# Seven more blocks and one recurrence result of a two-layer fp32 kernel turned by VectorE and ScalarE instead of TensorE

## The chip, the cores and the metric

The kernel runs on one core of a Trainium2 chip. The metric is the device time of one execution in microseconds (us). Before the change it is 2432.59 us, the median of three runs (2432.58 to 2432.67).

## What is computed

A sequence of 256 tokens with 2048 features passes through two layers, all in fp32. The first layer is a gated recurrence beside a short convolution, an output projection, and a feed-forward part. The second is conditioned by a vector (`ada`) and has two attentions, an output projection and a feed-forward part. Cut to what matters here:

```
# first layer
proj = rms(x) @ w_in                    # q, f forward, f backward, i, gate, b, c, h: 1024 columns each
y_rec  = rms(recurrence(silu(q), gates(f forward), gates(f backward), i)) * hgrn_norm_w * silu(gate)
y_conv = b * conv3(c * h)
x = x + concat(y_rec, y_conv) @ w_out ;  x = x + ffn(x) ;  x = rms(x)
# second layer
proj = h @ w_in_2                       # c_q (512), c_kv (512), k_pe (64), q_sb, k_sb, v_sb, two gates
q  = (rms(c_q) * g_q_latent) @ w_uq     # 8 heads of 128 "nope" and 64 "rope" columns
kv = (rms(c_kv) * g_kv_latent) @ w_ukv  # 8 heads of 128 k_nope and 128 v
y_a = attention(rms(q) * g_q_head, rms(k) * g_k_head, v)     # with rope on the 64 columns
y_b = stick_breaking(q_sb, k_sb, v_sb)
x = x + gt1 * ((sigmoid(gl_a) * (y_a @ w_mla) + sigmoid(gl_b) * (y_b @ w_sb)) @ w_out_2) ;  x = x + gt2 * ffn(x)
```

## The kernel before

**The stream of weights.** Every large product is cut into blocks of 512 output columns, each block into chunks of 256 rows of its weight (a chunk is 128 partitions x 1024 numbers, two rows of tiles). A chunk comes by DMA into one of four `raw` buffers. ScalarE (ACT) rounds it to fp32r in `cast` (L994, tile `whi`), VectorE (DVE) computes what the rounding left in `low` (L1418, `wlo`), and TensorE (PE) multiplies in `products` (L957 to L959): for each of two row tiles and two token halves `hi*whi + hi*wlo + lo*whi`, 12 matmuls of 512 columns. One such chunk on PE is a **visit**; there are 913, numbered from 0. Each engine runs one instruction stream written out by hand. Slot s of a stream belongs to visit s: PE does `side_work(s)` and then the products of visit s, ACT does its `side_work(s)` and then the cast of chunk s+3, DVE the low part of that chunk at the start of its slot s+1, before its own `side_work(s+1)`. So between the slot in which a chunk is cast and the visit that needs it lie three visits. Nothing is reordered at run time; a late instruction delays all behind it on its engine.

**Turning.** A finished block lies with tokens on partitions; for the next product or attention it must have features there. Two ways are in use. On PE: `turn` (L664), a transposition of 128 x 128, 8 for a block, into PSUM, from where ACT and DVE read it. Without PE, for blocks that `is_far` names: `turned` on DVE (L1759), two STREAM_TRANSPOSE of 128 x 512, which turn each square of 32 x 32 in itself, into the rows of `between(b)`; then 16 copies of 32 partitions x 256 (`piece`, L1035 on ACT, L1506 on DVE), which put the squares in their places in `features_at(b)`. `pace(b)` says how many pieces a slot has on ACT and on DVE, (3, 0) as a rule. `live(s)` gives the blocks whose side work is due: `t` counts slots from the end of the block, up to `LIFE`.

**The places of this change.** Visits 16 to 23 are the block `fb` (the backward gate's input) of group 0 of the recurrence; its half steps follow in `hgrn(g, u)`, where u counts slots from `H0[g]` (slot 30 for group 0, 94 for group 1), with seven levels three slots apart; its result is normed, gated and turned at u = 33 to 37 and used by block `out` from visit 128 on. Visits 428 to 447 are the two latent blocks of the second layer; 457 to 462 the blocks `uqr` and `nope` q0, q1; 471 to 474 `nope` k0, k1; 475 to 478 the values `uv`; from 479 on the four blocks `heads` of the second attention. A `nope` block is evacuated at t = 0 (L1150), squared at t = 1 (L1156), summed at t = 2 (L1690 and after), scaled by its norm at t = 4 (L1712), turned at t = 6 and scaled by its gain as ACT takes it out of PSUM (L1163). The first attention's head h has its scores at slot `MLA0 + 3h`, that is from slot 485 on.

```
def cast(c):                      # ACT
    if pl.after[c] is not None:
        e.wait_ge(*visit(pl.after[c]))       # the visit that frees the buffer
    ...
    e.copy(whi[i][:, :, :], raw[u % RAW][:, 2 * hf:2 * hf + 2, :])
for s in range(SLOTS):            # ACT
    side_work(s)
    for c in pl.visits[s][2]:
        cast(c)
```

Of the kernel before, what the change touches and what calls it, by code (L numbers as in the profile page):

```python
# [29 lines left out]
LIFE = 14  # L30
# [262 lines left out]
def two_block_kernel(nc, a, out):  # L293
    ctx = ExitStack()
    with ctx:
# [221 lines left out]

        def as_features(t):

            return flat(t).rearrange("p (k s) -> p k s", k=4)  # L520
# [24 lines left out]
        H0 = [pl.end("fb", g) + 6 for g in range(2)]  # L545
# [3 lines left out]
        MLA0 = pl.begin("heads", "qs", 0) + 6  # L549
# [18 lines left out]
        FAR = (("fup", None), ("sb", 3), ("out", 3), ("heads", None), ("q", None), ("ff", None), ("h", 1), ("b", 1))  # L568
# [25 lines left out]
        def between(b):  # L594

            if b.kind in ("fup", "sb", "out"):
                return FT[:, :, :]
            if b.kind == "heads":
                return gl[0][:, :, :] if b.arg == ("ks", 1) else T2[1 - b.index % 2][:, :, :]
            k0 = 8 if (b.kind, b.arg[0]) == ("ff", 0) else 12  # L600
            return way[k0][:, :, :]

        def features_at(b):

            n = b.arg[-1]
            if b.kind in ("fup", "sb", "out"):
                return as_features(T2[n % 2][:, :, :])
            if b.kind == "heads":
                return (qs if b.arg[0] == "qs" else ks)[:, 4 * n:4 * n + 4, :]
            if b.kind == "q":  # L610
                return qT[:, :].rearrange("p (k s) -> p k s", k=4)
            if b.kind == "ff":
                return Kx[:, 0, :].rearrange("p (k s) -> p k s", k=4)
            if b.kind == "h":
                return U[:, :, 1:S + 1]
            return bT[:, :, :]
# [6 lines left out]

        def piece(b, q, i):

            d = features_at(b)[32 * q:32 * q + 32, :, :].rearrange("p k (m i c) -> p m i k c", m=2, i=4)
            r = between(b)[32 * i:32 * i + 32, :, :].rearrange("p m (k q c) -> p m q k c", k=4, q=4)
            return d[:, :, i, :, :], r[:, :, q, :, :]
# [33 lines left out]
        def tensor_program(e):  # L662
# [18 lines left out]
            def block_side(b, t):  # L681
# [20 lines left out]
                elif kind == "kpe" and t == 1:  # L702
                    e.wait_ge(*acc_read(b, 0))
                    o = next_bank(e, b.index)
                    for m in range(2):
                        ins = turn(o[:, P * m:P * m + P], ev_tmp(b, 0)[:, P * m:P * m + P])
                    ins.then_inc(*ev("pe_turn", b.index))
                elif kind == "nope" and t == 6:
                    for m in range(2):
                        e.wait_ge(*on("dve_nope", b.index, "scaled", m))  # L710
                        turn_tokens(b, m, (b.index, m))
                elif kind == "heads" and t == 2:
                    for m in range(2):
                        e.wait_ge(*acc_read(b, m))
                        turn_tokens(b, m, (b.index, m))
                elif kind == "sb" and t in (2, 3):
                    m, j = t - 2, b.arg[0]
                    e.wait_ge(*on("dve_merge", j, m))
                    o = next_bank(e, b.index, m)
                    for k in range(4):  # L720
                        ins = turn(o[:, P * k:P * k + P], ffn_tmp(j, m)[:, P * k:P * k + P])
                    ins.then_inc(*ev("pe_turn", b.index, m))

            def hgrn(g, u):
# [34 lines left out]
                elif u in (35, 36):  # L759
# [49 lines left out]
            def side_work(s):  # L809
# [10 lines left out]
                for g in range(2):  # L820
                    if 0 <= s - H0[g] < 40:
                        hgrn(g, s - H0[g])
# [61 lines left out]
            def left_here(b, i, ci, m):  # L884
# [5 lines left out]
                elif b.kind == "out" and b.arg == (0,) and i == 0 and m == 0:  # L890
                    if kt < 8:
# [18 lines left out]
                elif (b.kind == "uqr" or b.kind == "nope" and b.arg == ("k", 0)) and i == 0 and m == 0:  # L910
                    e.wait_ge(*side_read(pl.at["latent", 0 if b.kind == "uqr" else 1].index, ci))
# [60 lines left out]
        def scalar_program(e):  # L972
# [38 lines left out]
            def block_side(b, t):  # L1011
# [18 lines left out]
                elif is_far(b) and 2 <= t < settled(b):  # L1030
                    if t == 2:
                        for m in range(2):
                            e.wait_ge(*on("dve_turned", b.index, m))
                    for q, i in pieces(b, t, "act"):
                        ins = e.copy(*piece(b, q, i))  # L1035
                    if last_piece(b, t, "act"):
                        ins.then_inc(*ev("act_moved", b.index))
                elif is_far(b) and kind == "ff" and t == settled(b):
                    e.wait_ge(*on("act_moved", b.index))
                    e.activation(TA[:, 1024:2048], Kx[:, 0, :], ACT.Sigmoid, bias=0.0, scale=1.0).then_inc(  # L1040
                        *ev("act_gate", b.index, "f"))
                    e.activation(Kx[:, 0, :], Kx[:, 0, :], ACT.Sigmoid, bias=0.0, scale=-1.0).then_inc(
# [6 lines left out]
                elif is_far(b) and kind == "out" and t in (8, 9):  # L1049
                    half, k0 = t - 8, 4 * b.arg[0]  # L1050
                    if half == 0:
                        await_moves(e, b)
                    for k in (2 * half, 2 * half + 1):
                        ins = e.activation(hH[:, k0 + k, :], features_at(b)[:, k, :], ACT.Copy, bias=0.0,
                                           scale=vc("ffn_norm_w", k0 + k))
# [4 lines left out]
                elif is_far(b) and t >= 2 and kind != "out":  # L1060
# [97 lines left out]
                elif kind == "nope" and t == 6:  # L1158
# [19 lines left out]
                elif kind == "gl" and t == (3 if b.arg[0] == 3 else 0):  # L1178
                    i = b.arg[0]
                    e.wait_ge(*visit(end))  # L1180
                    if i == 0 and is_far(pl.at["heads", "ks", 1]):
                        await_moves(e, pl.at["heads", "ks", 1])
# [19 lines left out]
            def hgrn(g, u):  # L1202
# [21 lines left out]
                elif u in (35, 36):  # L1224
# [27 lines left out]
            def side_work(s):  # L1252
                for b, t in live(s):
                    block_side(b, t)
                for g in range(2):
                    if 0 <= s - H0[g] < 40:
# [141 lines left out]
        def vector_program(e):  # L1398
# [97 lines left out]
            def block_side(b, t):  # L1496
                kind, end = b.kind, pl.last[b.index, 1]
                t -= late0(b)
                if is_far(b) and t == 1:
                    turned(b)  # L1500
                elif is_far(b) and 2 <= t < settled(b) and pace(b)[1]:
                    if t == 2:
                        for m in range(2):
                            e.wait_ge(*on("dve_turned", b.index, m))
                    for q, i in pieces(b, t, "dve"):
                        ins = e.tensor_copy(*piece(b, q, i))  # L1506
                    if last_piece(b, t, "dve"):
                        ins.then_inc(*ev("dve_moved", b.index))
                elif is_far(b) and kind in ("fup", "sb") and t == settled(b) + 1:
# [3 lines left out]
                elif is_far(b) and kind == "out" and t in (9, 10):  # L1513
                    half, k0 = t - 9, 4 * b.arg[0]
                    e.wait_ge(*on("act_half", b.index, half))
                    for k in (2 * half, 2 * half + 1):
                        ins = e.scalar_tensor_tensor(hL[:, k0 + k, :], features_at(b)[:, k, :], vc("ffn_norm_w", k0 + k),
                                                     f(hH[:, k0 + k, :]), ALU.mult, ALU.subtract)
# [131 lines left out]
                elif kind == "latent" and t == 5:  # L1650
# [94 lines left out]
            def turned(b):  # L1745

                for m in range(2):
                    if b.kind == "sb":
                        e.wait_ge(*on("dve_merge", b.arg[0], m))
                    elif b.kind == "out":  # L1750
                        e.wait_ge(*on("dve_x1", b.index, m))
                    else:
                        e.wait_ge(*acc_read(b, m))
                if (b.kind, b.arg) == ("heads", ("ks", 1)):
                    e.wait_ge(*on("pe_head", "mla", 7, "y"))
                elif b in users:
# [79 lines left out]
            def hgrn(g, u):  # L1836
# [52 lines left out]
                elif u in (36, 37):  # L1889
# [204 lines left out]
            def side_work(s):  # L2094
# [4 lines left out]
                for g in range(2):  # L2099
                    if 0 <= s - H0[g] < 40:  # L2100
# [280 lines left out]
```

## Time and profile before

| | |
|---|---|
| median of three runs | 2432.59 us |
| the profiled execution | 2432.96 us |
| its span, first to last instruction | 2431.1 us |
| PE busy | 2424.0 us, 11540 matmuls |
| DVE busy | 1794.2 us |
| ACT busy | 1411.8 us |
| granted clock of PE | 1.00 |
| PE in the chain that ended last | 99% |

The profiled execution takes 1.9 us more than its span: what lies before the first and after the last instruction. Matmuls overlap in the pipeline, so that one of 512 columns is shown as 379 ns long while the next starts 216 ns after it; PE's speed is read from starts. The engines' busy shares are averages over the whole program.

### The profile page before, as it was taken

The page shows a single profiled execution, that of the slowest core. Times are in us where ns is not written, and L with a number is a line of the kernel's source. Part 1 is how long each engine was busy: PE and PEld are TensorE (multiplying, and loading weights), DVE is VectorE, ACT ScalarE, POOL GpSimd, SP SyncE. Part 2 cuts the span into 40 slices and gives each one's busy share as a digit, 9 for nine tenths or more (in the row PEclk, how much of TensorE's full clock was granted, in tenths as well). Part 3 has the DMA queues.
Part 4 walks back from the last instruction along what each step waited for, and adds up shares of the span by engine and source line. Part 5 has one row for each costly group of instructions (what it writes and reads, how often), then busy time and mean ns, then how long its engine had stood idle before and what let it go on. Part 6 is the DMA issues. An engine that isn't in the chain of part 4 may idle for free.

```text
span 2431.1 us, 29441 instructions
## 1 busy us (share of the span) xinstructions
PE 2424.0 (100%) x11540; PEld 2125.4 (87%) x11540; DVE 1794.2 (74%) x2231; ACT 1411.8 (58%) x1980; POOL 26.0 (1%) x27
## 2 busy tenths in 40 slices
PE   9999999999999999999999999999999999999999
PEld 8898888888888888888888888888888888888888
DVE  7888798777778778786666666789778775555555
ACT  7647645756654455655766664465656564455643
POOL 0000000000000000000010000000000000000000
PEclk9999999999999999999999999999999999999999
DMA  8656667787778877786455456878577776556564
GB/s 306 242 193 233 234 213 254 247 292 274 271 267 311 308 263 276 271 291 218 168 190 173 163 173 241 291 254 298 190 277 278 278 275 208 202 199 205 203 205 146
DMA packets 83321, 582.38 MB, mean 240 GB/s; under 512 B 9712, under 2 KB 10096, under 8 KB 13552
## 3 DMA queue, kind: packets, MB, share of 16 engines
q1 hardware_dynamic: 83040, 580.39, 67.2%
q8 instruction: 91, 1.49, 0.2%
q14 instruction: 46, 0.38, 0.0%
q10 hardware_dynamic: 144, 0.12, 0.0%
HBM read 578.36 MB, written 2.11 MB: 239 GB/s over the span
## 4 chain that ended last, share of the span: by engine, by line
PE 99%; DMA 0%; DVE 0%; ACT 0%; SPq 0%; issue 0%; POOL 0%; ACTq 0%
PE bank L957 32%; PE bank L958 32%; PE bank L959 32%; PE bank L738 1%; PE bank L664 1%; DMA raw<-in_w_in_dram 0%; PE bank L776 0%; PE bank L787 0%; PE bank L788 0%; PE bank L757 0%; PE bank L746 0%; PE bank L756 0%; PE bank L777 0%; PE bank L804 0%; PE bank L940 0%; PE bank L941 0%
## 5 line engine op out<-in xcount | busy, mean ns | idle before, releaser
L1418 DVE TENSOR_TENSOR wlo<-raw,whi 128x1024 fp32r<-128x1024 f32 x885 | 1077.5, 1221 | 554.2 <-ACT whi L994 550.0
L994 ACT CAST whi<-raw 128x1024 fp32r<-128x1024 f32 x885 | 926.3, 1048 | 756.4 <-PE bank L959 742.4
L957 PE MATMUL bank<-whi,hH 128*128 128x512 f32 x2528 | 967.8, 383 | 1.3 <-DVE wlo L1418 1.2
L958 PE MATMUL bank<-wlo,hH 128*128 128x512 f32 x2528 | 958.1, 379 | 0.0
L959 PE MATMUL bank<-whi,hL 128*128 128x512 f32 x2528 | 958.1, 379 | 0.0
L957 PEld LDWEIGHTS bank<-whi,hH 128*128 128x128 f32 x2528 | 478.0, 189 | 68.9 <-DVE wlo L1418 2.0
L959 PEld LDWEIGHTS bank<-whi,hL 128*128 128x128 f32 x2528 | 477.8, 189 | 67.8
L958 PEld LDWEIGHTS bank<-wlo,hH 128*128 128x128 f32 x2528 | 478.0, 189 | 65.8
L1924 DVE SCALAR_TENSOR_TENSOR adacc<-raw,stat,adacc 128x512 f32<-128x512 f32 x360 | 269.6, 749 | 6.8
L957 PE MATMUL bank<-whi,aH 128*128 128x512 f32 x704 | 267.1, 379 | 0.1
L958 PE MATMUL bank<-wlo,aH 128*128 128x512 f32 x704 | 266.8, 379 | 0.0
L959 PE MATMUL bank<-whi,aL 128*128 128x512 f32 x704 | 266.8, 379 | 0.0
L1035 ACT COPY two<-turned 32x256 f32<-32x256 f32 x432 | 174.1, 403 | 32.1 <-DVE turned L1759 25.0
L957 PEld LDWEIGHTS bank<-whi,aH 128*128 128x128 f32 x704 | 133.1, 189 | 19.3 <-issue 0.4
L959 PEld LDWEIGHTS bank<-whi,aL 128*128 128x128 f32 x704 | 133.1, 189 | 19.0
L958 PEld LDWEIGHTS bank<-wlo,aH 128*128 128x128 f32 x704 | 133.1, 189 | 18.6
L957 PE MATMUL bank<-whi,mH 128*128 128x512 f32 x128 | 48.7, 380 | 0.0
L958 PE MATMUL bank<-wlo,mH 128*128 128x512 f32 x128 | 48.5, 379 | 0.0
L959 PE MATMUL bank<-whi,mL 128*128 128x512 f32 x128 | 48.5, 379 | 0.0
L2165 POOL TENSOR_TENSOR stat<-stat 128x4 f32<-128x4 f32 (+2 forms) x22 | 24.0, 1100 | 1705.0 <-DVE stat L1438 990.9
L1759 DVE STREAM_TRANSPOSE turned<-two 128x512 f32<-128x512 f32 x50 | 32.4, 686 | 0.0
L1628 DVE TENSOR_TENSOR two<-bank,two 128x512 f32<-128x512 f32 x44 | 28.3, 684 | 3.6 <-PE bank L959 3.6
(331 smaller groups left out, 1514.5 us busy)
## 6 DMA issues: line engine op xcount, KB each, us to landing
raw<-in_w_gu_dram SPq DMA_DIRECT2D x176, 1024.0 KB, 4.9
raw<-in_w_ada_dram SPq DMA_DIRECT2D x96, 1024.0 KB, 4.9
raw<-in_w_down_dram SPq DMA_DIRECT2D x88, 1024.0 KB, 4.9
raw<-in_w_in_dram SPq DMA_DIRECT2D x60, 1024.0 KB, 4.8
raw<-in_w_in2b_dram SPq DMA_DIRECT2D x56, 1024.0 KB, 4.8
raw<-in_w_out_dram SPq DMA_DIRECT2D x32, 1024.0 KB, 4.9
raw<-in_w_in2a_dram SPq DMA_DIRECT2D x8, 1024.0 KB, 4.8
raw<-in_w_mla_dram SPq DMA_DIRECT2D x8, 1024.0 KB, 4.8
```

The lines of the kernel that those rows point to most:

```text
L664: return e.transpose(o, i, ident[0:n, 0:n])
L738: ins = e.matmul(o[:, P * hd:P * hd + P], KC[:, base:base + P], qq, start=True, stop=True)
L957: e.matmul(o, xh[:, kt, sl], pairs(wh, i), start=k == 0, stop=False)
L958: e.matmul(o, xh[:, kt, sl], pairs(wl, i), start=False, stop=False)
L959: ins = e.matmul(o, xl[:, kt, sl], pairs(wh, i), start=False, stop=k == n - 1)
L994: e.copy(whi[i][:, :, :], raw[u % RAW][:, 2 * hf:2 * hf + 2, :]).then_inc(*ev("act_hi", c, 0))
L1035: ins = e.copy(*piece(b, q, i))
L1418: e.tensor_tensor(wlo[i][:, :, :], raw[u % RAW][:, 2 * hf:2 * hf + 2, :], f(whi[i][:, :, :]), ALU.subtract).then_inc(*ev("dve_lo", c, 0))
L1628: e.tensor_tensor(d, summed(b, m), d, ALU.mult).then_inc(*acc_free(b, m))
L1759: e.transpose(between(b)[:, m, :], rows_at(b)[:, m, :]).then_inc(*ev("dve_turned", b.index, m))
L1924: ins = e.scalar_tensor_tensor(d, src, col, d, ALU.mult, ALU.add)
L2165: e.tensor_tensor(sc(o, n), sc(i, n), sc(b_half, n), ALU.pow).then_inc(*ev("pool_pow", *key))
```

## The change

Block `fb` of group 0, both latents, the four `nope` blocks q0, q1, k0, k1, and the result of the recurrence of group 0, which PE turned, are now turned by DVE and moved by ACT (for `fb` and k1 also by DVE): eight blocks of 256 tokens x 512 features, 64 transpositions of PE. `lag(b)` starts a latent's turning at t = 3 and a `nope`'s at t = 5 or 9. The gain of a `nope` is applied by one 128 x 1024 ACTIVATE after the pieces; a latent's and the recurrence's gain and split read the turned block in SBUF. `H0[0]` moves from slot 30 to 33, the first attention's heads from slot 485 to 487. PE waits for the new events (`act_gain`, `dve_low`) where it waited for a PSUM bank before. On DVE the pieces of a block now stand before its transpositions in the text. No DMA is added or moved.

```diff
-LIFE = 14
+LIFE = 18
...
-        H0 = [pl.end("fb", g) + 6 for g in range(2)]
+        H0 = [pl.end("fb", 0) + 9, pl.end("fb", 1) + 6]
...
-        MLA0 = pl.begin("heads", "qs", 0) + 6
+        MLA0 = pl.begin("heads", "qs", 0) + 8
...
-        FAR = (("fup", None), ("sb", 3), ("out", 3), ("heads", None), ("q", None), ("ff", None), ("h", 1), ("b", 1))
+        FAR = (("fup", None), ("sb", 3), ("out", 3), ("heads", None), ("q", None), ("ff", None),
+               ("h", 1), ("b", 1), ("fb", 1), ("latent", None), ("nope", None))
...
         def pace(b):
 
+            if b.kind == "fb":
+                return 3, 1
+            if b.kind == "nope" and b.arg == ("k", 1):
+                return 2, 1
...
-                return gl[0][:, :, :] if b.arg == ("ks", 1) else T2[1 - b.index % 2][:, :, :]
+                return as_rows(qr[:, 0:4, :]) if b.arg == ("ks", 1) else T2[1 - b.index % 2][:, :, :]
+            if b.kind == "nope":
+                return {("q", 0): as_rows(qs[:, 0:4, :]), ("q", 1): as_rows(qs[:, 4:8, :]), ("k", 0): gl[2][:, :, :],
+                        ("k", 1): as_rows(ks[:, 4:8, :])}[b.arg]
+            if b.kind == "latent":
+                return gl[1 + b.arg[0]][:, :, :]
...
+        def lag(b):
+
+            return 2 if b.kind == "latent" else 4 + 4 * b.arg[1] if b.kind == "nope" else 0
...
-                elif kind == "nope" and t == 6:
+                elif kind == "nope" and t == 6 and not is_far(b):
...
-                elif u in (35, 36):
+                elif u in (35, 36) and g == 1:
...
+                    if h % 4 == 0:
+                        for which in ("q", "k"):
+                            e.wait_ge(*on("act_gain", pl.at["nope", which, h // 4].index))
...
-                elif is_far(b) and 2 <= t < settled(b):
-                    if t == 2:
+                elif is_far(b) and 2 <= t - lag(b) < settled(b):
+                    if t == 2 + lag(b):
                         for m in range(2):
                             e.wait_ge(*on("dve_turned", b.index, m))
...
+                elif is_far(b) and kind == "nope" and t - lag(b) == settled(b):
+                    await_moves(e, b)
+                    e.activation(features_at(b), features_at(b), ACT.Copy, bias=0.0,
+                                 scale=vc("g_q_nope" if b.arg[0] == "q" else "g_k_nope")).then_inc(*ev("act_gain", b.index))
...
+                elif g == 0 and 55 <= u < 63:
+                    if u == 55:
+                        for m in range(2):
+                            e.wait_ge(*on("dve_turned", "hturn", m))
+                    for k in (2 * u - 110, 2 * u - 109):
+                        ins = e.copy(*quadrant(*mixed_way(), *divmod(k, 4)))
...
+                elif g == 0 and u == 34:
+                    for m in range(2):
+                        e.wait_ge(*on("dve_hgrn", g, "gated", m))
+                    for m in range(2):
+                        e.transpose(mixed_way()[1][:, m, :], T2[0][:, m, :]).then_inc(*ev("dve_turned", "hturn", m))
```

**ACT in slots 467 to 471**, the first five slots in which block `nope` q0 (turned) is moved into `qn`. `CAST whi` is the stream's cast, `qr` the rope part taken from PSUM, `vs` the evacuation of a value block. Before:

```order
L1163 ACTIVATE qn<-bank,vec 128x4x128 x2
L994 CAST whi_55<-raw_52 128x1024
L994 CAST whi_56<-raw_49 128x1024
L1163 ACTIVATE qn<-bank,vec 128x4x128 x2
L994 CAST whi_53<-raw_49 128x1024
L1282 COPY qr<-bank 64x4x128
L1283 COPY qr<-bank 64x4x128
L994 CAST whi_54<-raw_50 128x1024
L1137 COPY vs<-bank 128x512 x2
L1282 COPY qr<-bank 64x4x128
L1283 COPY qr<-bank 64x4x128
L994 CAST whi_55<-raw_50 128x1024
```

And in the change:

```order
L1076 COPY qn<-qs 32x2x4x32 x3
L1035 CAST whi_55<-raw_52 128x1024
L1076 COPY qn<-qs 32x2x4x32 x3
L1035 CAST whi_56<-raw_49 128x1024
L1076 COPY qn<-qs 32x2x4x32 x3
L1035 CAST whi_53<-raw_49 128x1024
L1076 COPY qn<-qs 32x2x4x32 x3
L1341 COPY qr<-bank 64x4x128
L1342 COPY qr<-bank 64x4x128
L1035 CAST whi_54<-raw_50 128x1024
L1076 COPY qn<-qs 32x2x4x32 x3
L1183 COPY vs<-bank 128x512 x2
```

Two ACTIVATEs from PSUM in every second slot become three pieces in every slot, ahead of what the slot had. The same pattern goes on to slot 490, with k0 and k1 behind q1.

**DVE in slots 65 to 67**, in which the convolution of group 0 (`tmp<-U`) falls; `two<-bank,stat` is the norm of the recurrence's result, `two<-two,Gg` its gate, `way<-two` the turning of block `b`. Before:

```order
L1572 TENSOR_SCALAR tmp_79<-U,vec 128x128 x2
L1575 SCALAR_TENSOR_TENSOR tmp_79<-U,vec,tmp_79 128x128 x4
L1759 STREAM_TRANSPOSE way_87<-two_77 128x512 x2
L1418 TENSOR_TENSOR wlo_57<-raw_50,whi_53 128x1024
L1572 TENSOR_SCALAR tmp_80<-U,vec 128x128 x2
L1575 SCALAR_TENSOR_TENSOR tmp_80<-U,vec,tmp_80 128x128 x4
L1432 SCALAR_TENSOR_TENSOR mL<-bank,vec,mH 128x256 x2
L1418 TENSOR_TENSOR wlo_58<-raw_50,whi_54 128x1024
L1572 TENSOR_SCALAR tmp_80<-U,vec 128x128 x2
L1575 SCALAR_TENSOR_TENSOR tmp_80<-U,vec,tmp_80 128x128 x4
L1432 SCALAR_TENSOR_TENSOR mL<-bank,vec,mH 128x256 x2
L1418 TENSOR_TENSOR wlo_59<-raw_51,whi_55 128x1024
```

And in the change:

```order
L1631 TENSOR_SCALAR tmp_79<-U,vec 128x128 x2
L1634 SCALAR_TENSOR_TENSOR tmp_79<-U,vec,tmp_79 128x128 x4
L1822 STREAM_TRANSPOSE way_87<-two_77 128x512 x2
L1944 TENSOR_TENSOR two_76<-bank,stat 128x512 x2
L1477 TENSOR_TENSOR wlo_57<-raw_50,whi_53 128x1024
L1631 TENSOR_SCALAR tmp_80<-U,vec 128x128 x2
L1634 SCALAR_TENSOR_TENSOR tmp_80<-U,vec,tmp_80 128x128 x4
L1950 TENSOR_TENSOR two_76<-two_76,Gg 128x512 x2
L1477 TENSOR_TENSOR wlo_58<-raw_50,whi_54 128x1024
L1631 TENSOR_SCALAR tmp_80<-U,vec 128x128 x2
L1634 SCALAR_TENSOR_TENSOR tmp_80<-U,vec,tmp_80 128x128 x4
L1956 STREAM_TRANSPOSE TB<-two_76 128x512 x2
```

The norm, the gate and the turning of the recurrence's result, which stood three slots earlier or on PE, now stand in the slots of the convolution.

## Rows read from the trace of the kernel before

**Rows 1.** The page: span, busy time of the engines.

```profile
span 2431.1 us, 29441 instructions
PE 2424.0 (100%) x11540; PEld 2125.4 (87%) x11540; DVE 1794.2 (74%) x2231; ACT 1411.8 (58%) x1980; POOL 26.0 (1%) x27
```

**Rows 2.** Waits of PE, the longest in total: us, times, longest.

```profile
PE bank L957 <- DVE wlo L1418: 1.2, 2, 1.0
```

**Rows 3.** The chain that ended last, in order of time: start us, us, what.

```profile
79.79 0.44 PE bank L664 x4
...
1255.10 0.87 PE bank L664 x8
```

**Rows 4.** Line L664: duration ns min/median/max, first and last start.

```profile
L664 PE MATMUL bank<-ident,two x170: 272/273/329, 76.6 to 1757.2; 128*128 128x128 f32 x170
```

**Rows 5.** Timelines of ACT and DVE: start us, us, what; a slot with three pieces.

```profile
207.07 1.23 ACT L1035 COPY bT<-way 32x256 f32<-32x256 f32 x3
208.31 1.05 ACT L994 CAST whi<-raw 128x1024 fp32r<-128x1024 f32 x1
...
202.64 1.29 DVE L1759 STREAM_TRANSPOSE way<-two 128x512 f32<-128x512 f32 x2
203.86 1.18 DVE L1418 TENSOR_TENSOR wlo<-raw,whi 128x1024 fp32r<-128x1024 f32 x1
```

**Rows 6.** DVE and PE, slot 26 to visit 28.

```profile
79.66 1.22 DVE L1418 TENSOR_TENSOR wlo<-raw,whi 128x1024 fp32r<-128x1024 f32 x1
...
82.66 0.38 PE L957 MATMUL bank<-whi,hH 128*128 128x512 f32 x1
```

**Rows 7.** PE at the start of slot 60, then DVE in slots 61 to 65.

```profile
184.42 0.38 PE L756 MATMUL bank<-Vv,ST 128*128 128x128 f32 x2
...
187.97 1.23 DVE L1418 TENSOR_TENSOR wlo<-raw,whi 128x1024 fp32r<-128x1024 f32 x1 [2.21 <-ACT whi L994]
...
190.56 0.68 DVE L1875 TENSOR_REDUCE stat<-two 128x4 f32<-128x512 f32 x1
...
191.36 1.22 DVE L1418 TENSOR_TENSOR wlo<-raw,whi 128x1024 fp32r<-128x1024 f32 x1
...
196.28 1.29 DVE L1887 TENSOR_TENSOR two<-two,Gg 128x512 f32<-128x512 f32 x2
197.48 1.22 DVE L1418 TENSOR_TENSOR wlo<-raw,whi 128x1024 fp32r<-128x1024 f32 x1
198.62 0.47 DVE L1572 TENSOR_SCALAR tmp<-U,vec 128x128 f32<-128x128 f32 x2
...
200.06 1.21 DVE L1418 TENSOR_TENSOR wlo<-raw,whi 128x1024 fp32r<-128x1024 f32 x1
```

**Rows 8.** PE at the start of slot 467 and of slot 482.

```profile
1254.94 1.04 PE L664 MATMUL bank<-ident,two 128*128 128x128 f32 x8
...
1298.17 0.60 PE L664 MATMUL bank<-ident,tmp 128*128 128x128 f32 x4
```

**Rows 9.** DVE: the end of slot 465, and slot 477.

```profile
1255.76 2.35 DVE L1418 TENSOR_TENSOR wlo<-raw,whi 128x1024 fp32r<-128x1024 f32 x2
...
1283.67 1.29 DVE L1712 TENSOR_TENSOR two<-two,stat 128x512 f32<-128x512 f32 x2
...
1286.52 2.35 DVE L1418 TENSOR_TENSOR wlo<-raw,whi 128x1024 fp32r<-128x1024 f32 x2
```

**Rows 10.** ACT's other work: a gain-sized pass, slot 471, squares.

```profile
73.22 1.05 ACT L1040 ACTIVATE TA<-Kx 128x1024 f32<-128x1024 f32 x1
...
1267.69 1.08 ACT L1137 COPY vs<-bank 128x512 f32<-128x512 f32 x2 [0.35 <-PE bank L959]
1268.65 0.58 ACT L1282 COPY qr<-bank 64x512 f32<-64x512 f32 x1
...
1269.85 1.99 ACT L994 CAST whi<-raw 128x1024 fp32r<-128x1024 f32 x2
...
1280.40 1.16 ACT L1156 ACTIVATE square<-two 128x512 f32<-128x512 f32 x2
```

More of the change, by code:

```diff
@@ L1048, in block_side @@
                         e.copy(mH[:, k0:k0 + 4, P * m:P * m + P], v4(T[5 + m])).then_inc(*ev("act_half", b.index, m))
-                elif is_far(b) and kind == "out" and t in (8, 9):
-                    half, k0 = t - 8, 4 * b.arg[0]
+                elif is_far(b) and kind in ("out", "latent") and t - lag(b) in (8, 9):
+                    half, (hi, _, k0, gname) = t - lag(b) - 8, scaled_halves(b)
                     if half == 0:
@@ L1157, in block_side @@
                             *ev("act_sq", b.index, m))
-                elif kind == "nope" and t == 6:
+                elif kind == "nope" and t == 6 and not is_far(b):
                     which, n = b.arg
@@ L1223, in hgrn @@
                         *ev("act_sq", "hout", g, m))
-                elif u in (35, 36):
+                elif g == 0 and 55 <= u < 63:
[4 more added lines that the diff above has]
+                        ins = e.copy(*quadrant(*mixed_way(), *divmod(k, 4)))
+                    if u == 62:
+                        ins.then_inc(*ev("act_moved", "hturn"))
+                elif g == 0 and u in (63, 64):
+                    if u == 63:
+                        e.wait_ge(*on("act_moved", "hturn"))
+                    for k in (2 * u - 126, 2 * u - 125):
+                        ins = e.activation(mH[:, k, :], mixed_way()[0][:, k, :], ACT.Copy, bias=0.0,
+                                           scale=vc("hgrn_norm_w", k))
+                    ins.then_inc(*ev("act_half", "hturn", u - 63))
+                elif g == 1 and u in (35, 36):
                     scaled_high(mH, ("hturn", g, u - 35), 4 * g + 2 * (u - 35), "hgrn_norm_w")
@@ L1498, in block_side @@
                 t -= late0(b)
[L1499 to L1502, printed above, removed]
+                if is_far(b) and 2 <= t - lag(b) < settled(b) and pace(b)[1]:
+                    if t == 2 + lag(b):
                         for m in range(2):
                             e.wait_ge(*on("dve_turned", b.index, m))
[L1505 removed]
+                    for q, i in pieces(b, t - lag(b), "dve"):
                         ins = e.tensor_copy(*piece(b, q, i))
[L1507 removed]
+                    if last_piece(b, t - lag(b), "dve"):
                         ins.then_inc(*ev("dve_moved", b.index))
+                if is_far(b) and t - lag(b) == 1:
+                    turned(b)
                 elif is_far(b) and kind in ("fup", "sb") and t == settled(b) + 1:
@@ L1649, in block_side @@
                         *ev("dve_mean", "latent", i))
-                elif kind == "latent" and t == 5:
+                elif kind == "latent" and t == 5 and not is_far(b):
                     i = b.arg[0]
@@ L1751, in turned @@
                         e.wait_ge(*on("dve_x1", b.index, m))
+                    elif b.kind == "latent":
+                        e.wait_ge(*on("act_lat", b.index, m))
+                    elif b.kind == "nope":
+                        e.wait_ge(*on("dve_nope", b.index, "scaled", m))
                     else:
                         e.wait_ge(*acc_read(b, m))
-                if (b.kind, b.arg) == ("heads", ("ks", 1)):
-                    e.wait_ge(*on("pe_head", "mla", 7, "y"))
-                elif b in users:
+                if (b.kind, b.arg) == ("heads", ("qs", 0)):
+                    await_moves(e, pl.at["nope", "k", 0])
+                elif b in users and b.kind != "nope":
                     await_moves(e, users[b])
```

75 lines of the change are left out of this document (48 added, 27 removed).

## The prediction

> **What bounds the kernel now.** I read the page first: PE is busy for 2424.0 of 2431.1 us [rows 1]. Then PE's waits: the longest sort adds up to 1.2 us [rows 2]. So the time is the sum of what PE has to do; an instruction taken from PE is worth its time on PE, as long as ACT and DVE still deliver each chunk before its visit. That second half is what this change puts at risk, because ACT (1411.8 us) and DVE (1794.2 us) are far from idle, and their load is not spread evenly. So the timelines of the three engines in the slots that the change touches come next, read for starts, since durations overlap.
>
> A visit takes PE 2.59 us: between the starts of slots 467 and 482 lie 43.23 us [rows 8], less four groups of eight transpositions and two of four, over 15 visits. ACT's and DVE's deadline is this: chunk s+3, cast in slot s, must be through `low` when visit s+3 begins. If it isn't, PE waits.
>
> **What is removed.** 64 transpositions. One is shown as 272 ns long [rows 4], but a group of eight holds the chain for 0.87 us and one of four for 0.44 [rows 3], 0.109 each, because they overlap. Six groups of eight (latents, `nope`) and four of four (`fb`, the recurrence's result): 6 x 0.875 + 4 x 0.44 = **7.0 us** off PE. The instruction order shows exactly these gone from PE, and no other work added there; SP, POOL and the DMAs have the same instructions as before. Without waits the profiled execution would take 2432.96 - 7.0 = 2426.0 us.
>
> **What is added.** For each of the eight blocks DVE gets two STREAM_TRANSPOSE, 1.22 us from start to start of what follows [rows 5], and ACT 16 pieces, three in 1.24 us [rows 5], 6.6 us together. A `nope` also gets a gain pass, about 0.95 (the row of such a pass shows 1.05 with its overlap [rows 10]), and loses two reads of PSUM. So 0.87 us of the full engine is exchanged for 7.8 us on two engines with room on average. The Trainium skill (VectorE: DVE Perf Modes, Rules for kernel authors) advises TensorE for a 128 x 128 transposition whose result may go to PSUM, and DVE for 32 x 32 within a bank. By its advice the kernel before is the better one; the rows side with it wherever ACT or DVE has no room, and against it elsewhere. I go through the places in turn.
>
> *`fb`, slots 25 to 33.* The low part for visit 28 starts on DVE at 79.66 and takes 1.22; PE begins visit 28 at 82.66 [rows 6]. Two transpositions now stand ahead of it: it ends at 79.66 + 1.22 + 1.22 = 82.1. PE without eight transpositions would begin at 82.66 - 0.88 = 81.8. Wait: **0.3 us**. From there to visit 33, ACT has three pieces and DVE one in each slot, then ACT two sigmoid passes; reckoned in the same way the chunks are 0.1 to 0.6 us early, so I take nothing; the bounds are 0 and 1 us.
>
> *The recurrence's result, slots 63 to 70.* It moves by three slots into those of the convolution. What was slot 60 is slot 63. From PE's start of it DVE begins a low part after 187.97 - 184.42 = 3.55 us [rows 7], and ends it at 4.7. Up to and with the low part for visit 70, DVE then has: four convolution parts of 1.44 (198.62 to 200.06), a reduction with its scaling 0.8, norm and gate 1.2 each (196.28 to 197.48), four low parts (three of 1.14, the last 1.22 to its end) [rows 7], two pairs of transpositions of 1.22 [rows 5]: 4.7 + 5.8 + 0.8 + 2.4 + 4.6 + 2.4 = 20.7. PE gets to visit 70 after seven visits and 16 small matmuls (0.11 each): 18.1 + 1.8 = 19.9. Wait: **0.8 us**; bounds 0 and 1.5. Behind it DVE has two light slots. The pieces of this result come in slots 88 to 97, two a slot, 0.8 us of ACT; visit 88 and those after it have chunks some 5 us early, so nothing.
>
> *Latents, slots 443 to 460.* The slots are light on both engines. The pieces end five slots before `uqr`. Nothing.
>
> *`nope`, slots 466 to 482.* This is the place that decides. DVE is late already: it starts its low part for visit 468 and the next together at 1255.76 [rows 9]. The transpositions of q0 follow the first, so they end at 1258.2. ACT waits for them: its pieces of slot 467 begin 3.3 us after the slot's start at 1254.94 [rows 8]. From then on it never catches up. Its work from there to the cast of slot 479: 35 pieces at 0.413 = 14.5; 13 casts at 1.05 = 13.7; two gain passes 1.9; five evacuations at 0.96 = 4.8 and two pairs of `qr` copies at 1.20 = 2.4 (1267.69, 1268.65, 1269.85) [rows 10]; two pairs of squares, 1.16 less an overlap of 0.1 [rows 10], 2.1. Sum 39.4. Add one wait in slot 479 for DVE: slot 477 costs DVE 2.85 us (1283.67 to 1286.52) [rows 9] ahead of a low part and the transpositions of k0, which end 0.8 us after ACT is ready. And add the last low part, 1.25. In all 41.5 us. PE, without the four groups of eight, has 43.23 - 3.50 = 39.7 us from slot 467 to slot 482. Wait by then: 3.3 + 41.5 - 39.7 = **5.1 us**, begun at visit 474 and taken in pieces of 0.4 to 1.4 us. Bounds: 1.8 us if ACT somehow starts slot 467 in time (5.1 - 3.3), 6.6 if DVE's transpositions hold ACT up twice more by 0.8. I take 5.1, since each term is a row's. From slot 480 on the slots of ACT are shorter than PE's and there is 0.7 us of slack again, then 1.3.
>
> *The first attention, two slots on.* Scores wait for the gains of q0 and k0, given in slot 485, two slots before; those of q1 and k1 in slot 491, eight before. The second attention's and the gates' deadlines have slack of several slots. Nothing; the cover is ACT's slack of 1.2 us at slot 485.
>
> **Sum.** -7.0 + 0.3 + 0.8 + 5.1 = -0.8 us: 2432.96 - 0.8 = 2432.2 for a profiled execution. The median of the runs is 0.4 below the profiled one: **2431.8 us**.
>
> **The rivals.** About 0.2% (4.9 us) is what a measurement of this kernel can tell from no change.
>
> *The cover holds.* ACT and DVE absorb most of it: waits of 0 to 2 us, time 2425.6 to 2427.7, say 2426.5, faster. For it: on average both have room (58% and 74%), and the head start of three chunks has hidden similar bunches, PE's waits being near zero. Against it: the `nope` chain is a sum of busy time in order, with one start fixed by DVE, and 13 slots of ACT can't borrow from elsewhere. It decides if the waits stay under 2.1 us.
>
> *PE gets back more per transposition.* The trace shows them 0.109 us apart. The Trainium skill (TensorE: Matmul & The Clock Gate, Part 4: PE-mode transpose) has about 275 ns for one in a kernel's context; the 272 ns of rows 4 agree as a duration, not as a cost. If each really kept PE for the 272 ns, 64 of them were 17.4 us, and with the cover holding the time 2415. The starts speak against it.
>
> *Slower: ACT's lateness reaches the heads.* In slots 485 to 491 ACT has gain passes, pieces of k1 and of `heads` and the first exponentials at once. If it enters late and each of the eight heads then costs PE a wait of the size of the `nope` chain's pieces, 0.8 us or more beyond the slack of 1.2, 8 x 0.8 - 1.2 = 5.2 us come on top: 2437. Under 0.8 a head it doesn't turn the sign past 0.2%. For it: seven slots there hold about 21 us of ACT's work in 21 us of PE's. Against it: the heads' own small matmuls make PE's slots longer as ACT's get heavier.
>
> That the change doesn't do what it says is excluded by the order of the instructions.
>
> **How the numbers follow.** The walk through the slots: 0.76 (it includes waits from 2.1 us up). The cover holds: 0.15. PE gets back more: 0.01. Slower: 0.08. Its own range for the likeliest is 2430 to 2434, from the bounds: waits of 4.4 to 8.4 us. The lower bounds of all places (1.8 in `nope`, 0 elsewhere) reach to 2427.4; 2427.5 to 2434.5 leaves out most of the faster case and the slower one. Faster by over 0.2%, under 2427.7: 0.16; slower, above 2437.5 or close to it: 0.07; within 0.2%: 0.77.
>
> **What the profile would show.** Right: L664 on PE 64 fewer; PE idle some 6 us, released by DVE `wlo`; one short wait at visit 28, one at visit 70, the rest between visits 474 and 482; ACT's pieces `qn<-qs` starting 3 us into slot 467 and ACT without idle time from there to slot 479. Wrong: waits under 2 us in all; or ACT idle between slots 468 and 478; or waits in the slots of the heads; or a group of eight worth other than 0.87 us where nothing waits.

## The result, and the profile after

The changed kernel takes **2439.0 us**, the median of eight runs (2436.6 to 2440.9), beside 2432.65 us (2432.3 to 2432.9) for the kernel before: a ratio of 1.0026, 95% interval 1.0016 to 1.0035. It is 6.3 us slower, more than the 4.9 us below which the prediction would have called it no change. Forecast were 2431.8 us and no change, with 0.07 for slower.

The page of the profiled execution (2440.93 us) answers to [rows 1]:

```profile
span 2439.0 us, 29459 instructions
...
PE 2421.5 (99%) x11476; PEld 2119.1 (87%) x11476; DVE 1806.9 (74%) x2256; ACT 1462.3 (60%) x2093; POOL 26.0 (1%) x27
```

There are 64 matmuls fewer, as intended, but the span is 7.9 us longer. PE's waits (us in total, times, longest), to be held against the 1.2 us of [rows 2]:

```profile
PE bank L998 <- DVE wlo L1477: 3.7, 6, 1.1
PE bank L700 <- DVE tmp L2190: 3.3, 1, 3.3
PE bank L700 <- DVE tmp L2184: 2.0, 1, 2.0
PE bank L998 <- ACT vm L1183: 1.2, 1, 1.2
PE bank L1005 <- DVE ones_r L2214: 1.1, 1, 1.1
...
PE bank L998 <- ACT two L1196: 0.5, 1, 0.5
...
PE bank L998 <- DVE aL L1571: 0.4, 1, 0.4
```

`ones_r` was there before. L998 is the stream's product (L957 before), and `wlo` the wait that the prediction looked for. The two longest waits are for something else: L700 (L664 before) is `turn`, `tmp` is the rope part of q (L2184) or of k (L2190), which DVE scales and PE then turns in slots 470, 471, 482 and 483. The prediction counted ACT's copies of that result (`qr`) and never asked when PE needs the product. PE around the two waits (start us, us, what, idle before and its releaser):

```profile
1261.72 0.38 PE L1000 MATMUL bank<-whi,hL 128*128 128x512 f32 x1
1264.06 0.66 PE L700 MATMUL bank<-ident,tmp 128*128 128x128 f32 x4 [1.96 <-DVE tmp L2184]
...
1298.82 0.38 PE L1000 MATMUL bank<-whi,hL 128*128 128x512 f32 x1
1302.50 1.11 PE L700 MATMUL bank<-ident,tmp 128*128 128x128 f32 x4 [3.30 <-DVE tmp L2190]
1303.27 0.78 PE L998 MATMUL bank<-whi,hH 128*128 128x512 f32 x1
1303.84 0.63 PE L999 MATMUL bank<-wlo,hH 128*128 128x512 f32 x1
1304.26 0.63 PE L1000 MATMUL bank<-whi,hL 128*128 128x512 f32 x1
```

and DVE and ACT ahead of the second:

```profile
1299.54 1.05 ACT L1035 CAST whi<-raw 128x1024 fp32r<-128x1024 f32 x1
1300.61 1.24 ACT L1076 COPY kn<-gl 32x256 f32<-32x256 f32 x3
...
1298.30 1.22 DVE L1477 TENSOR_TENSOR wlo<-raw,whi 128x1024 fp32r<-128x1024 f32 x1 [1.08 <-ACT whi L1035]
1300.62 1.23 DVE L1477 TENSOR_TENSOR wlo<-raw,whi 128x1024 fp32r<-128x1024 f32 x1 [1.10 <-ACT whi L1035]
1301.76 0.69 DVE L2190 TENSOR_TENSOR tmp<-kpe,stat 128x512 f32<-128x512 f32 x1
```

The product's inputs were ready before (`kpe` since 1219.8, the norm, which POOL finishes, since 1295.5). It is late because it stands on DVE behind a low part that waited for ACT's cast. That low part is the one of visit 483, which PE needs only after all products of visit 482. Before the change, the same rows:

```profile
1261.89 0.68 DVE L2110 TENSOR_TENSOR tmp<-tmp,stat 128x512 f32<-128x512 f32 x1
...
1294.77 0.68 DVE L2116 TENSOR_TENSOR tmp<-kpe,stat 128x512 f32<-128x512 f32 x1
```

They ended at 1262.57 and 1295.45, and PE turned them from 1264.46 and from 1298.17 (the second in [rows 8]): slack of 1.9 and 2.7 us. In the changed kernel the first ends 1.4 us later (1264.00) and PE comes 2.5 us earlier (the last product of visit 469 starts at 1261.72, one spacing of 0.22 before): 1.4 + 2.5 - 1.9 = 2.0 us of wait. The second ends 7.0 us later and PE comes 0.9 later: 7.0 - 0.9 - 2.7 = 3.4.

ACT's lateness reaches PE in a third way, without DVE. A block begins in the PSUM bank of the block before the last, and PE waits until ACT has copied that one out, which stands in the slot two visits ahead (`sem_acc` in `products`). At visits 477 and 479 this copy ends last (the 0.5 and 1.2 us above), after the low part:

```profile
1283.79 0.45 PE L998 MATMUL bank<-whi,ckH 128*128 128x512 f32 x1 [0.51 <-ACT two L1196]
1290.45 0.45 PE L998 MATMUL bank<-whi,hH 128*128 128x512 f32 x1 [1.20 <-ACT vm L1183]
...
1288.48 1.23 DVE L1477 TENSOR_TENSOR wlo<-raw,whi 128x1024 fp32r<-128x1024 f32 x1 [2.14 <-ACT whi L1035]
```

The low part of visit 479 was ready at 1289.71, 0.7 us before PE could start.

After the second wait for the rope the products of slot 482 start 0.43 us apart instead of 0.216. Windows of the same execution (us, then PE, PEld, DVE, ACT, POOL busy, granted clock, DMA share, GB/s):

```profile
1298.00:1302.00 4.00, 1.20 (x6) 0.71 (x4) 2.60 (x3) 3.88 (x9) 0.00 (x0) 0.95 0.37 86
1302.00:1306.00 4.00, 3.50 (x11) 2.96 (x12) 2.41 (x4) 3.89 (x7) 0.00 (x0) 0.50 0.63 213
1306.00:1310.00 4.00, 4.00 (x16) 3.27 (x15) 1.10 (x1) 1.91 (x5) 0.00 (x0) 0.69 0.55 229
```

The granted clock fell while PE waited (0.95 in the first window) and was at its lower level (0.50, that is 1.2 GHz) through slot 482. Neither ACT nor DVE held PE up in that slot; from the start of its transpositions it took 6.00 us, 3.03 before.

**Where the time went**, visit by visit from the starts of PE in both profiled executions: 64 transpositions -7.0; waits at visits 28 to 34 +0.7; at 70 and 71 +1.0; at visits 392 and 434 +0.55; slots 470 to 481 +5.1, of which 2.2 is the first wait for the rope; the second wait for it +3.5; the clock behind it +3.0; one wait near visit 618, which is 0.3 in e7's profile and under 0.1 in the others, +0.6; the start of the program +0.3, which moves by up to half a microsecond between the profiles of all kernels here. Sum +7.7, of 7.9.

### The profile page after: what moved, and what is told of

The parts are those of the page before. It is cut to its first block, busy times and chain, and to the rows that moved or that the text cites. A ratio compares the mean times of both kernels' runs of the same rounds, so it can differ in the third digit from the quotient of the medians.

```text
span 2439.0 us, 29459 instructions
## 1 busy us (share of the span) xinstructions
PE 2421.5 (99%) x11476; PEld 2119.1 (87%) x11476; DVE 1806.9 (74%) x2256; ACT 1462.3 (60%) x2093; POOL 26.0 (1%) x27
## 4 chain that ended last, share of the span: by engine, by line
PE 52%; DVE 2%; ACT 2%; issue 1%; DMA 0%; POOL 0%; ACTq 0%
PE bank L998 17%; PE bank L1000 17%; PE bank L999 17%; DVE wlo L1477 1%; ACT whi L1035 1%; PE bank L700 1%; DVE adacc L1998 0%; ACT qn L1076 0%; DMA raw<-in_w_out_dram 0%; PE bank L812 0%; PE bank L826 0%; PE bank L827 0%; PE bank L813 0%; PE bank L843 0%; DVE stat L1749 0%
## 5 line engine op out<-in xcount | busy, mean ns | idle before, releaser
L998 PE MATMUL bank<-whi,hH 128*128 128x512 f32 x2528 | 968.9, 383 | 5.4 <-DVE wlo L1477 3.7
L998 PEld LDWEIGHTS bank<-whi,hH 128*128 128x128 f32 x2528 | 478.5, 189 | 76.2 <-DVE wlo L1477 8.2
L998 PE MATMUL bank<-whi,aH 128*128 128x512 f32 x704 | 267.1, 379 | 0.4 <-DVE aL L1571 0.4
L998 PEld LDWEIGHTS bank<-whi,aH 128*128 128x128 f32 x704 | 133.1, 189 | 19.6 <-issue 0.7
L998 PE MATMUL bank<-whi,mH 128*128 128x512 f32 x128 | 48.7, 380 | 0.0
```

Source lines behind the costliest of these rows:

```text
L998: e.matmul(o, xh[:, kt, sl], pairs(wh, i), start=k == 0, stop=False)
```

## The experiments

Theory A: all of the loss is the four `nope` blocks', and most of it the rope products standing on DVE behind late low parts, with the clock's fall after the longer wait. Theory B: ACT's 40 us chain sets the time, wherever PE waits. Each kernel was timed over 10 or 11 runs beside the kernel before. The 95% intervals allow for more than the scatter of these runs. Those of e1 and e5 contain 1, although their ranges lie wholly below that of the kernel before; the ranges of e3, e6 and e9 overlap it, and for them the text also goes by the starts of PE in the traces.

| run | median us (range) | before | ratio, 95% |
|---|---|---|---|
| e1 without `nope` | 2431.67 (2431.1 to 2432.2) | 2432.78 | 0.9995 (0.9986 to 1.0004) |
| e2 `nope` alone | 2438.8 (2437.8 to 2440.2) | 2432.78 | 1.0025 (1.0016 to 1.0034) |
| e3 rope late | 2434.0 (2433.2 to 2434.6) | 2432.78 | 1.0005 (0.9996 to 1.0014) |
| e4 busy wait | 2436.67 (2436.4 to 2437.1) | 2432.78 | 1.0016 (1.0007 to 1.0025) |
| e5 latents alone | 2430.99 (2430.7 to 2431.4) | 2432.83 | 0.9993 (0.9984 to 1.0002) |
| e6 `fb`, recurrence | 2433.59 (2433.3 to 2434.1) | 2432.83 | 1.0003 (0.9994 to 1.0012) |
| e7 rope late, shared | 2430.34 (2430.1 to 2431.1) | 2432.83 | 0.9991 (0.9982 to 0.9999) |
| e8 and turned later | 2430.09 (2429.7 to 2431.4) | 2432.83 | 0.9989 (0.9980 to 0.9998) |
| e9 one more on ACT | 2433.0 (2432.6 to 2433.4) | 2432.69 | 1.0001 (0.9993 to 1.0010) |
| e10 latents and `nope` | 2429.59 (2429.2 to 2429.9) | 2432.69 | 0.9987 (0.9978 to 0.9996) |
| e11 one slot later | 2429.58 (2429.3 to 2430.1) | 2432.69 | 0.9987 (0.9978 to 0.9996) |
| e12 shared alone | 2435.32 (2433.6 to 2436.1) | 2432.69 | 1.0009 (1.0000 to 1.0018) |

**e1, the change without `nope`.**

```diff
-               ("h", 1), ("b", 1), ("fb", 1), ("latent", None), ("nope", None))
+               ("h", 1), ("b", 1), ("fb", 1), ("latent", None))
-        MLA0 = pl.begin("heads", "qs", 0) + 8
+        MLA0 = pl.begin("heads", "qs", 0) + 6
```

> The change without its four nope blocks (heads at +6 again): fb, the recurrence's result and the latents are turned without TensorE. Theory A (all that is lost comes from nope): 32 transpositions fewer, -3.5 us, with the waits seen in the changed kernel at visits 27 to 33 (+0.8) and 69 and 70 (+1.05): 2432.6 - 3.5 + 1.85 = 2430.9. Theory C (the gain of 0.109 us per transposition is not real, or these places cost more than their waits): 2432.5 or more.

Measured 1.1 us faster than before, where theory A's sum has 1.65. The missing 0.55 is explained below (e6, e9).

**e2, `nope` alone.** The kernel before with the four `nope` blocks of the change and its `MLA0`.

> The kernel before with only the four nope blocks (and the heads two slots on) of the change. Theory A: -3.5 + 9.6 to 11.6 us, 2438.7 to 2440.7, slower than the whole change is, with waits for L2184 and L2190 (rope products on VectorE) of about 2 and 3.3 us. Theory C (the places add to each other): under 2437.

Measured 2438.8, as theory A said: 32 transpositions fewer and 6 us slower.

**e3, the rope turned two slots later.**

```diff
-                for which, base in (("q", QR0 + 11), ("k", QR0 + 23)):
+                for which, base in (("q", QR0 + 13), ("k", QR0 + 25)):
```

(on PE and on ACT.)

> The whole change, with TensorE's turning of the rope parts and ScalarE's copies of them two slots later (q from slot 470 to 472, k from 482 to 484), nothing else moved. Theory A (TensorE waits for rope products that stand on VectorE behind a low part that waits for a late cast; the clock falls in that wait): both waits and the fall go, waits for wlo at visits 476 to 482 grow by at most 2 us; 2434.5, between 2433 and 2436, clock 1.000. Theory B (ScalarE's 40 us chain sets the time, whatever TensorE waits at): the wait only changes its place, over 2437.5.

2434.0: 5.0 us gained by an edit that moves 16 transpositions and their copies and takes no work away. The clock is 1.000 in all eleven runs, so its fall is part of the 5.0; against the change's one run at 1.000 the gain is 2.6. PE's waits:

```profile
PE bank L998 <- DVE wlo L1477: 4.1, 6, 1.4
PE bank L998 <- ACT two L1196: 1.2, 1, 1.2
PE bank L998 <- ACT vm L1183: 1.2, 1, 1.2
```

None of them is for `tmp`. Theory B is refuted for the loss as a whole, but it holds for what is left: from visit 475 to 482 PE now waits 5.5 us at its products, where the prediction had reckoned 5.1. About half of that, at visits 477 and 479, waits for ACT's copies out of PSUM and not for `wlo`. That the product stands behind the low part on DVE is read from the trace; putting it ahead of the low part, the direct test, was not tried.

**e4, the second wait filled with work that counts for nothing.**

```diff
-                        e.wait_ge(*on("dve_rope", which, m))
                         o = next_bank(e, "rope", which, m)
+                        if (which, m) == ("k", 0):
+                            for _ in range(28):
+                                turn(o[:, 0:P], ident[:, :])
+                        e.wait_ge(*on("dve_rope", which, m))
```

> The whole change, with 28 extra transpositions of the identity (3.05 us of TensorE) in slot 482 ahead of the wait for L2190, into the bank that the real ones then overwrite. Theory A (the granted clock falls to 0.5 there because TensorE has idled, and 12 matmuls then take 5.1 us and not 2.6): the wait is spent on work that counts for nothing, the clock stays at 1.00, 2436 to 2437. If the clock's fall has another reason: the same as the change, 2439, clock under 1.000; if the extra work comes on top: 2440 or more.

2436.67, 2.3 us under the change, all eleven runs within 0.7 us. The windows behind the wait:

```profile
1302.00:1306.00 4.00, 4.00 (x24) 3.55 (x22) 2.78 (x3) 3.87 (x9) 0.00 (x0) 1.00 0.63 203
1306.00:1310.00 4.00, 4.00 (x21) 3.49 (x20) 2.30 (x4) 3.91 (x6) 0.00 (x0) 1.00 0.34 143
```

So idling was what let the clock fall. The clock in this profile is 0.999 nevertheless, since it fell behind the first rope wait, and slot 470 took 4.74 us:

```profile
1263.00:1267.00 4.00, 3.59 (x13) 2.97 (x14) 2.09 (x3) 3.90 (x7) 0.00 (x0) 0.65 0.60 190
```

That cost nothing in the end: the 1.7 us came off the waits at visits 477 and 479, where PE was held up by ACT anyway, and the five runs at 0.999 are within 0.2 us of the six at 1.000 in the median.

**e5 and e6, the other parts.** The kernel before with the two latents only; with `fb`, the recurrence's result and `H0[0]` only.

> The kernel before with only the two latent blocks turned without TensorE. Two groups of eight transpositions go, 1.75 us, in slots where nothing waits: 2432.7 - 1.75 = 2431.0 (0.25 more if the wait seen at slot 435 in the changed kernel and in e1 belongs to the latents). If a transposition gives back its 272 ns: 2428.4. If the exchange costs something elsewhere: 2432 or more.

> The kernel before with only block fb, the recurrence's result and the recurrence's three slots. -1.75 us of transpositions, +0.8 of waits at visits 27 to 33, +1.05 at visits 69 and 70: no net gain, 2432.7 (2432.4 to 2433.1). With e5 it adds to e1 if the parts are independent.

e5: -1.84 us, where sixteen transpositions at 0.109 make 1.75, and nothing else shows. e6: +0.76, not 0. Together -1.08, and e1 has -1.11: the parts add up. In e6's trace the waits at visits 28 to 34 are 0.7 and those at 70 and 71 1.0, as expected; on top come 0.31 and 0.25 us at visits 392 (called slot 391 in the expectations) and 434, some 700 us after the last instruction that the edit touches (see e9).

**e7, e3 with the pieces shared.**

```diff
-            if b.kind == "nope" and b.arg == ("k", 1):
+            if b.kind == "nope":
                 return 2, 1
```

> e3 (rope turned two slots later) with, in addition, the pieces of all four nope blocks shared, two a slot on ScalarE and one on VectorE. Theory (what is left of the loss in e3 is ScalarE's load): ScalarE gives 5 of 16 pieces of q0, q1 and k0, 15 x 0.41 = 6.2 us, VectorE takes them at 0.29; the 6 us of waits at visits 475 to 482 in e3 fall under 1 us: 2428.5 (2427.5 to 2429.5). If it is VectorE (or its late transpositions) that holds the chain: over 2432.

2430.34 is 3.7 us under e3, so ACT's load was most of what was left, but it is 1.8 over the expectation and outside its range. The waits at visits 475 to 478 are gone, 1.6 us at visit 480 and 0.5 around it are not.

**e8, and the recurrence's result turned a slot later** (`u == 34` becomes `u == 35` on DVE).

> e7 with, in addition, VectorE's two STREAM_TRANSPOSE of the recurrence's result one slot later (u = 35, behind the low part of visit 70 and not ahead of it). The wait of 1.05 us at visits 69 and 70 goes: 1.0 us under e7.

The medians differ by 0.25, not 1.0, and the ranges overlap. In the trace the 1.0 us at visits 70 and 71 went, and 0.5 us came at visits 75 and 76: half of the wait was only handed on.

**e9, one instruction more on ACT.**

```diff
-                    e.activation(sc(b_c, 16), vc("c", 0, 16), ACT.Sigmoid, bias=0.0, scale=1.0).then_inc(
+                    e.activation(sc(b_c, 8), vc("c", 0, 8), ACT.Sigmoid, bias=0.0, scale=1.0)
+                    e.activation(sc(b_c + 8, 8), vc("c", 8, 8), ACT.Sigmoid, bias=0.0, scale=1.0).then_inc(
```

> e6 with one ACTIVATE of 16 columns in ScalarE's slot 10 cut into two of 8, so that every later instruction of ScalarE stands one place further in its stream. In e6, and not in the kernel before, two waits of TensorE at slots 391 and 434 (0.31 and 0.25 us) go back to a ScalarE instruction that starts 0.33 to 0.35 us after its release instead of 0.06; both are number 63 modulo 64 in ScalarE's stream. If that place in the stream is the cause, both waits go: 2433.6 - 0.55 = 2433.0. If the wait belongs to what these instructions read or wait for: no change, 2433.6.

2433.0, 0.6 us less than e6 with one instruction more. ACT at its slot 390 in the kernel before, in e6 and in e9:

```profile
1066.50 1.05 ACT L1059 CAST aH<-two 128x1024 fp32r<-128x1024 f32 x1 [0.71 <-DVE two L1506]
```

```profile
1066.57 1.05 ACT L1105 CAST aH<-two 128x1024 fp32r<-128x1024 f32 x1 [1.02 <-DVE two L1567]
```

```profile
1066.47 1.05 ACT L1105 CAST aH<-two 128x1024 fp32r<-128x1024 f32 x1 [0.72 <-DVE two L1568]
```

The idle time ahead of this cast is 0.3 us longer in e6 alone. Both waits, at 392 and 434, are gone in e9, and one of 0.28 is new, at visit 647: ACT's instruction there in the kernel before and in e9:

```profile
1744.31 0.46 ACT L1368 ACTIVATE aux<-bank,adaF,stat 128x128 f32<-128x128 f32 x1 [0.34 <-PE bank L664]
```

```profile
1744.56 0.46 ACT L1432 ACTIVATE aux<-bank,adaF,stat 128x128 f32<-128x128 f32 x1 [0.61 <-PE bank L700]
```

The late instructions are numbers 1343 and 1471 in e6 and 2239 in e9, counted from zero with the waits that are instructions of their own. All three have the same place modulo 128 (see the last section): the late places stayed where they were in the stream and the work moved past them.

**e10, the two parts that pay**: `FAR` with latents and `nope`, without `fb`, recurrence and `H0[0]` as before, with e3's and e7's edits.

> The two parts that pay, together: latents and the nope blocks with the rope turned late and the pieces shared (as e7), and fb, the recurrence's result and the recurrence's slots as in the kernel before. If the parts are independent: e7 - 0.76 (what e6 lost) = 2429.6 (2429.2 to 2430.0).

2429.59 is the expected number, and with e11 the fastest version: 3.1 us under the kernel before, with ranges 2.4 us apart. PE's waits and DVE at what remains:

```profile
PE bank L996 <- DVE wlo L1460: 2.7, 3, 1.3
```

```profile
1283.48 1.23 DVE L1460 TENSOR_TENSOR wlo<-raw,whi 128x1024 fp32r<-128x1024 f32 x1 [1.18 <-ACT whi L1033]
1284.74 0.29 DVE L1546 COPY qn<-qs 32x256 f32<-32x256 f32 x1
1285.06 1.29 DVE L1754 TENSOR_TENSOR two<-two,stat 128x512 f32<-128x512 f32 x2
1286.27 1.27 DVE L1732 TENSOR_REDUCE stat<-square 128x4 f32<-128x512 f32 x2
...
1287.93 1.22 DVE L1460 TENSOR_TENSOR wlo<-raw,whi 128x1024 fp32r<-128x1024 f32 x1
```

The low part at 1287.93 is that of visit 480. It starts late through DVE's own 2.9 us of norms of k0 and k1 in one slot, behind a low part that ACT had already delayed.

**e11, q0 and k0 turned a slot later still.**

```diff
-            return 2 if b.kind == "latent" else 4 + 4 * b.arg[1] if b.kind == "nope" else 0
+            return 2 if b.kind == "latent" else 5 + 3 * b.arg[1] if b.kind == "nope" else 0
```

> e10 with the turning of q0 and k0 one slot later. In e8's profile ScalarE waits 4.7 us for the transpositions of q0 and 1.45 for those of k0 with its cast behind them, and TensorE then waits 1.6 us at slot 480 and 0.7 up to 483. Theory (a cast behind a piece that waits for a late VectorE is what is left): about 1.5 us less than e10, 2428.1. If it is VectorE's own load in slots 477 to 479: no change, 2429.6.

No change (2429.58). The waits at visits 479 to 482 are the same within 0.25 us each. ACT's wait for the transpositions was not what is left; the other branch of the expectation, DVE's slots 477 to 479, fits. Moving one of the two norms of k was not tried.

**e12, shared pieces with the rope in its old slots.**

> The whole change with the pieces of all nope blocks shared with VectorE as in e7, but the rope parts turned in their old slots 470 and 482. Theory A (TensorE's wait there depends on what stands ahead of the rope product in VectorE's queue, not on ScalarE's load alone): waits of 1.5 to 2 us for L2184 and for L2190, of which about 1.6 is saved again at slot 480; 2432.5 (2431.5 to 2433.5). If ScalarE's load alone made the loss: as e7, 2430.4.

2435.3 is neither e7's 2430.3 nor the expected 2432.5.

```profile
PE bank L700 <- DVE tmp L2190: 2.9, 1, 2.9
...
PE bank L700 <- DVE tmp L2184: 1.8, 1, 1.8
```

Theory A's sign holds: with 15 pieces fewer on ACT the rope waits are still 1.8 and 2.9 us, and the clock falls again behind the second (slot 482: 4.77 us). The expectation had priced only the waits, and at 1.5 to 2 us each: the four runs with a clock of 1.000 took 2433.6 to 2433.9 us, above its range too.

## Why the prediction was wrong

- **What is removed: right.** e5 gives 0.115 us per transposition, within its error of the 0.109 from the spacing. The rival with 272 ns each is refuted (it gave e5 2428.4). This also weighs the Trainium skill (TensorE: Matmul & The Clock Gate, Part 4: PE-mode transpose): its 275 ns is a latency here, too, and no price in a stream.
- **`fb`: 0.3 us forecast, 0.7 measured**, inside the bounds of 0 to 1. The wait at visit 28 was 0.5, with PE's slower restart behind it. I took the 0.1-us margins after it for nothing; at visits 29 and 33 they turned into waits of 0.1 each.
- **The recurrence's result: 0.8 forecast, 1.0 measured.** The sum over DVE's slots was right.
- **Latents: nothing forecast, nothing measured.**
- **`nope`, ACT's chain: right, and right in size.** ACT's pieces began 3.3 us into slot 467 (1257.51 against 1254.17), it then ran without idling to 1294.4, and the waits up to slot 481 add up to 5.1 us, as forecast; in e3, without the rope's waits, those up to 482 add up to 5.5. The places were not those forecast. In the changed kernel 2.2 of the 5.1 us are the rope's wait at slot 470, 2.2 end with ACT's copies out of PSUM (visits 477 and 479) and 0.7 with a low part (visit 480). The sum holds because each of these waits sets PE back to ACT's pace, wherever it falls.
- **The step that failed** is the first part's deadline: "chunk s+3, cast in slot s, must be through `low` when visit s+3 begins. If it isn't, PE waits." This is one of three ways in which ACT's lateness reaches PE. DVE executes in order (the rows of L2190 above), so a low part that waits for a late cast also holds what stands behind it. That low part is for the visit two slots on, but the rope product behind it is read in the very next slot. By the chunks the cover was three visits from the cast, by the rope 1.9 and 2.7 us. [Rows 8] name the rope product's reader: the end of my stretch, 1298.17, is PE's `bank<-ident,tmp`. I used the row as a clock mark and did not ask who makes `tmp`. The second rope wait cost 3.5 us that were missing in the sum (the first, 2.2, took the place of waits that I had). The third way is ACT's copy out of PSUM, two visits ahead of its reader, which the prediction counted as ACT's work and not as something that PE waits for.
- **The clock** was in no term and no bound. It cost 3.0 us in the profiled execution, and most of the spread between the runs goes with it. Of the eight the one with a clock of 1.000 took 2436.6 us, the others, at 0.998 or 0.999, 2438.6 to 2440.9. Even without it the time was 2.1 us above my range.
- **The slower rival** gave 2437 but for another cause: no head shows a wait. The chance of 0.08 for slower stood on a mechanism that did not occur. Nor was there a term for what a shifted stream alone can cost, 0.55 us (e9). None of the listed signs of being wrong came: there was none for a wait on anything but a low part.

## What to carry to other kernels

When an engine is made later, follow every queue that it feeds, not only the product that it is meant to feed: list for each engine that will stall on it what stands behind the stalled instruction, who reads that, and how soon, and list what the late engine itself hands to the bottleneck. The smallest of those slacks is the bound: here a reader one slot away mattered before the head start of three. Where a wait remains on the bottleneck engine, move its reader later in that engine's order before taking work from anyone (5.0 us here for no work saved, about half of it the clock's), and then share the load by measuring parts alone: of three parts one paid in full (e5), one cost more than it gave (e6), and one paid only after its reader was moved and its pieces were shared (e7, e10). Either alone was not enough (e3, e12).

## What was not expected of the hardware

- **The clock fell in some executions only.** In e2, with the same wait of 3.3 us, five runs show 1.000 (2437.8 to 2438.3 us) and five 0.998 or 0.999 (2439.3 to 2440.2): 1.6 us between the medians of the halves. Where a profile caught the fall, it lasted for all or part of one slot, and the slot took 3.0 us longer (482 in the change) or 1.7 (482 in e12, 470 in e4). The Trainium skill says that transpositions do not count as work for this clock in the way of matmuls (TensorE: Matmul & The Clock Gate, Part 4: PE-mode transpose). Here the trace doesn't bear that out for fp32: in e4 28 of them held the clock at 1.00 in slot 482, in the profile. One profile alone would prove little, since half of e2's runs kept the clock without them, but all eleven runs of e4 stayed within 0.7 us of each other, at the time of the change's one run at 1.000.
- **A place in ACT's stream costs 0.3 us.** Instructions 191, 703, 1343 and 1471 in e6, 2111 in e2 and 2239 in e9 started 0.32 to 0.33 us after the wait instruction ahead of them had ended, where 192, 704 and 1344 in e9, the same work one place further on, took 0.04. Each late one is 63 modulo 128, counted as above (e9's expectation had found 63 modulo 64, which these fulfil too). Not every such place is late: instruction 959 in e6, a cast that waits for PE itself and is released long after the wait instruction ahead of it, starts 0.02 us after its release. The Trainium skill (Runtime: NRT & Kernel Launch, Instruction fetch mechanics) has instructions fetched in blocks of 256 and the crossing mostly hidden; the numbers here repeat by 128, and whether fetching is the cause no run here shows.
